# A two-block network on one core: opening from free memory, gate products with the input moving, gate rows through DRAM, alternating banks

## The chip, the cores and the metric

The kernel is one program on one core of a Trainium2 chip. The metric is the time of the whole launch in microseconds (us), the median of several runs. Engines are named as in the profile: PE (TensorE matmul), DVE (VectorE), ACT (ScalarE), POOL (GpSimd), SP (SyncE, which here issues most of the loads). A row of the profile that begins with `ACTq` or `SPq` is a transfer that this engine issues.

## The reference

One sequence of S=512 tokens with D=1024 features goes through two blocks of two layers each, all in float32. Heads, softmaxes and recurrences are left out here; what matters is where linears, modulations and gates stand.

```
cs = silu(c)
ada = cs @ w_ada[i] + b_ada[i]                # 6 vectors of 1024 per layer
sh1, sc1, g1, sh2, sc2, g2 = split(ada, 6)
u = x * (1 + sc1) + sh1
proj = u @ m_w_in                             # q, k (2048), v, o (1024 each), 8 gate columns
y = mlstm(conv and silu of qk, v, o, gates) @ m_w_out
x = layer_norm(alpha * x + (1 + g1) * y)
u = x * (1 + sc2) + sh2
y = (gelu(g) * a) @ f_w_down                  # a, g = conv(u @ f_w_up), 2 * 2816 columns
x = layer_norm(alpha * x + (1 + g2) * y)
# then a second layer like it, with differential attention in place of the mLSTM cell
# second block: its own c_2, mod_w, mod_b; x = x + (1 + gt) * y with rms_norm ahead of each half
#   layer 0: RWKV7 time mix (r, k, v from three mixes of the same input), then a squared-relu MLP
#   layer 1: shared k, v and 16 gate columns, forgetting attention, then a squared-relu MLP
```

## The kernel before

Each engine has a program of its own, written out in order by hand; the only thing that moves work between them is semaphores (`wait_ge`). The stages follow each other as m (mLSTM), f0 (its feed-forward net), d (differential attention), f1, r (RWKV7), g0 (MLP), x (forgetting attention), g1 (MLP).

**Linears.** Weights come as tiles of 1 MB through three slots (`ring`), issued by SP, which waits for `used` of the tile three before. Each tile is split in two parts, `w_high` by ACT (`act_split`) and `w_low` by DVE (`dve_split`), two tiles ahead (`AHEAD = 2`). A product is three matmuls of 128x512 (high by high, high by low, low by high). A *turn* is two tiles of one linear: 96 such matmuls into banks 0 to 3 of PSUM. In a linear of kind "f" (`pe_linear_f`) the weight is the stationary side and the four sums of a turn come out one after another; in one of kind "t" (`pe_linear_t`) all four come out in the last piece. `act_evict`, `dve_beside`, `dve_residual` and `act_residual` are what ACT and DVE do in a turn; in all of them the split of the last piece stands behind the turn's evictions or residual.

**Modulation blocks.** `c @ w_ada` is 52 blocks of 1024x512 ("ada"), 2 MB each through two buffers (`ada_ring`). DVE multiplies and adds the eight row groups into `ada_acc` and adds the bias row, on one partition; PE then sums over partitions with four products of one column (`pe_ada`), and ACT copies four columns into `mod` (`act_ada`). Most blocks stand beside a turn. The first four stand ahead of everything in `ada_first`; the "1 +" of a scale is added by DVE in `dve_modulate`.

**Turned inputs.** `pe_turn` transposes the input into banks 4 to 7, ACT scales and shifts it into `stage`, and ACT and DVE write `u_high` and `u_low`.

**Gate products.** The 8 gate columns of m and the 16 of x are made by `pe_gates` between the turned input and the first linear: the input is the stationary side and 8 or 16 columns move, and the sums are transposed afterwards.

**Gate rows.** The residual needs `1 + g` as a row on all partitions. `pe_gate_rows` makes it with eight products of a broadcast column by the identity in front of each of the eight inputs that follow (m out, f0, d out, f1, r out, g0, x out, g1), and `dve_gate_rows` copies it with 1 added.

**Joins.** Between the stages, `join` makes every engine wait until all others have come to it.

Of the kernel before, what the change touches and what calls it, by code (L numbers as in the profile page):

```python
# [9 lines left out]
F32 = mybir.dt.float32  # L10
F32R = mybir.dt.float32r
# [3 lines left out]
P = 128  # L15
# [26 lines left out]
def shape_constants():  # L42
# [40 lines left out]
    ("c", 8), ("c_2", 8), ("m_conv_b", 16), ("m_norm_g", 8), ("d_norm_g", 8), ("norm_mix_g_2", 16),  # L83
    ("norm_mlp_g_2", 16), ("kv_norm_g_2", 8), ("f_conv_b", 88), ("m_conv_w", 64), ("rw_mu_2", 48),
    ("f_conv_w", 264),
]

# [34 lines left out]
class Queue:  # L122
# [60 lines left out]
    def dma_start(self, out, in_):  # L183
        return self.e.dma_start(out, in_) if self.live else QUIET
# [18 lines left out]
class Linear:  # L203


    def __init__(self, name, kind, w, turns, at, kts=KT, r0=0, ada=None):
# [5 lines left out]
        self.first = None  # L212
# [12 lines left out]
class Net:  # L225
    def __init__(self, nc, ctx, args, out, scratch):
        self.nc, self.a, self.out, self.scratch = nc, args, out, scratch
# [4 lines left out]
        self.ada_row_in = Signal(nc, "ada_row_in")  # L232
# [9 lines left out]
        self.signals = [self.T, self.V, self.A, self.G, *self.weights_in, *self.ada_in, self.ada_row_in,  # L242
                        self.params_in, self.core_in, self.x_in, self.stage_in, self.wkv_par_in,
# [5 lines left out]
    def layout(self):  # L249
# [19 lines left out]
        self.arow = take("ada_bias_row", [1, 512])  # L269
# [7 lines left out]
        self.rows = take("param_rows", [P, 5, P])  # L277
        ar.top = base
        self.stage = take("stage", [P, 2, S])
        self.u = [take(f"u_{x}", [P, KT, S], F32R) for x in ("high", "low")]  # L280
        lin = ar.top

# [5 lines left out]
        self.m_gw = self.gate_tiles("m", 8)  # L288
# [72 lines left out]
        self.x_gw = self.gate_tiles("x", 16)  # L361
# [12 lines left out]
    def gate_tiles(self, s, n):  # L374
        take = self.ar.take
        return [take(f"{s}_gw_raw", [P, KT, n]), take(f"{s}_gw_nat", [P, TT, n]),
                take(f"{s}_gw_high", [P, KT, n], F32R), take(f"{s}_gw_low", [P, KT, n], F32R)]
# [6 lines left out]
    def linears(self):  # L384
        a = self.a
        ada = {"a0": (a["w_ada"][0], a["b_ada"][0], 0, self.cs[:, 0:8]),
               "a1": (a["w_ada"][1], a["b_ada"][1], 48, self.cs[:, 0:8]),
               "m0": (a["mod_w_2"][0], a["mod_b_2"][0], 96, self.cs[:, 8:16]),
               "m1": (a["mod_w_2"][1], a["mod_b_2"][1], 144, self.cs[:, 8:16]),
               "kv": (a["kv_mod_w_2"], a["kv_mod_b_2"], 192, self.cs[:, 8:16])}  # L390
        self.ada_blocks = []

        def blocks(which, b0, n):
            w, b, col, cs = ada[which]
            first = len(self.ada_blocks)
            self.ada_blocks += [(w[:, (b0 + i) * 512:(b0 + i + 1) * 512], b[(b0 + i) * 512:(b0 + i + 1) * 512],
                                 col + 4 * (b0 + i), cs) for i in range(n)]
            return list(range(first, first + n))
# [37 lines left out]
        at = 0  # L436
        for x in lin:
            x.first = at
            at += x.turns * len(x.pieces)
        self.lin = {x.name: x for x in lin}  # L440
        self.weights = [tile for x in lin for tile in x.tiles()]
        self.break_at = self.lin["r_out"].first

# [32 lines left out]
    def sync_program(self, sp):  # L476
        a = self.a
        sp.dma_start(self.ident_t[:], a["core_constants"]).then_inc(*self.core_in.landed("core"))
        at = 0
        for name, n in COLUMN_PARAMS:  # L480
            src = self.row(name).rearrange("(r f) -> r f", f=P)
            done = 0
            while done < n:
                t, r = divmod(at, P)
                m = min(n - done, P - r)
                sp.dma_start(self.rows[r:r + m, t, :], src[done:done + m, :]).then_inc(*self.params_in.landed("rows"
                             if at + m == self.ncols else at))
                done += m
                at += m
        for b in self.ada_first:  # L490
            self.sp_ada(sp, b)
# [23 lines left out]

    def sp_linear(self, sp, name):
        L = self.lin[name]
        tiles = list(L.tiles())
# [2186 lines left out]
```

## Time and profile before

| | |
|---|---|
| median of 3 runs | 3668.22 us (3659.37 to 3672.21) |
| the profiled execution, own time | 3660.21 us |
| its span in the trace | 3658.9 us |
| PE busy | 3179.2 us, 87% of the span |
| DVE busy | 2089.3 us, 57% |
| ACT busy | 1121.9 us, 31% |
| mean granted clock of PE | 0.918 |
| bytes moved | 341.35 MB, mean 93 GB/s |

The span is from the first instruction to the last. The granted clock is a share of full speed: 1.00 is 2.4 GHz and 0.50 is 1.2 GHz. What is not PE's busy time, some 480 us, is idle time of PE between instructions.

### The profile page before, as it was taken

What the parts mean: (1) busy time and instruction counts of PE and PEld (TensorE: products, weight loads), DVE (VectorE), ACT (ScalarE), POOL (GpSimd) and SP (SyncE); (2) the same over time, 40 slices, a digit from 0 to 9 for tenths busy, and PEclk for the clock granted to TensorE, in tenths of its full rate; (3) what the DMA queues carried; (4) which work ended last, traced back from release to release, by engine and by line L of the source; (5) the groups of instructions that cost most, each with busy time, mean ns of one, the idle gap of its engine ahead of it and who ended that gap; (6) DMA issues with size and microseconds to landing.
All of it is one profiled execution on the core that took longest, in us unless ns stands there. A gap on an engine that the chain in (4) does not pass through costs nothing.

```text
span 3658.9 us, 46712 instructions
## 1 busy us (share of the span) xinstructions
PE 3179.2 (87%) x19829; PEld 2572.1 (70%) x19829; DVE 2089.3 (57%) x3089; ACT 1121.9 (31%) x1823; POOL 175.4 (5%) x137
## 2 busy tenths in 40 slices
PE   3989799996978799994978777689998998979998
PEld 3776688875845588872757677468887876768886
DVE  4655787776546686866346767345353153545353
ACT  1233242222234232322323434132123143433121
POOL 0000100001000100001003322000000001100000
PEclk8899899998979899997988998789999898989999
DMA  5552344643510354541210000113232121012332
GB/s 179 138 138 92 114 158 146 207 140 132 186 38 12 104 184 161 184 156 30 81 54 12 8 11 8 45 46 93 92 104 82 58 82 45 1 47 81 104 93 86
DMA packets 226684, 341.35 MB, mean 93 GB/s; under 512 B 11128, under 2 KB 113200, under 8 KB 226476
## 3 DMA queue, kind: packets, MB, share of 16 engines
q1 hardware_dynamic: 217484, 326.79, 27.7%
q10 hardware_dynamic: 8992, 11.58, 1.0%
q8 instruction: 156, 2.56, 0.3%
q14 instruction: 52, 0.43, 0.0%
HBM read 336.22 MB, written 2.12 MB: 92 GB/s over the span
## 4 chain that ended last, share of the span: by engine, by line
PE 70%; DVE 19%; ACT 6%; DMA 3%; issue 2%; SPq 0%; POOL 0%; ACTq 0%; DVEq 0%; POOLq 0%
PE bank L139 68%; DVE w_tiles L148 4%; DVE ada_acc L160 3%; PE bank L142 2%; DVE w_low L148 2%; DVE x_natural L148 1%; ACT w_high L145 1%; DVE m_acc L160 1%; ACT stage L145 1%; ACT small L145 1%; DMA weight_ring<-in_m_w_in 1%; DVE stage L148 1%; DVE u_low L148 1%; DVE w_g L148 1%; DVE f_g L160 0%
## 5 line engine op out<-in xcount | busy, mean ns | idle before, releaser
L148 DVE TENSOR_TENSOR w_low<-weight_ring,w_high 128x2048 fp32r<-128x2048 f32 (+2 forms) x212 | 463.1, 2189 | 573.5 <-ACT w_high L145 573.5
L139 PE MATMUL bank<-u_high,w_high 128*128 128x512 f32 x1472 | 580.1, 394 | 7.4 <-DVE w_low L148 7.1
L139 PE MATMUL bank<-u_low,w_high 128*128 128x512 f32 x1472 | 575.7, 391 | 0.0
L139 PE MATMUL bank<-u_high,w_low 128*128 128x512 f32 x1472 | 575.4, 391 | 0.0
L145 ACT ACTIVATE w_high<-weight_ring 128x2048 fp32r<-128x2048 f32 (+2 forms) x212 | 387.5, 1829 | 524.5 <-DMA weight_ring<-in_mlp_down 155.9
L139 PE MATMUL bank<-w_high,u_high 128*128 128x512 f32 x896 | 356.8, 398 | 23.6 <-ACT u_high L145 14.3
L139 PE MATMUL bank<-w_low,u_high 128*128 128x512 f32 x896 | 353.7, 395 | 0.0
L139 PE MATMUL bank<-w_high,u_low 128*128 128x512 f32 x896 | 353.3, 394 | 0.0
L139 PEld LDWEIGHTS bank<-u_high,w_high 128*128 128x128 f32 x1472 | 277.9, 189 | 67.2 <-DVE w_low L148 7.3
L139 PEld LDWEIGHTS bank<-u_high,w_low 128*128 128x128 f32 x1472 | 278.1, 189 | 59.2
L139 PEld LDWEIGHTS bank<-u_low,w_high 128*128 128x128 f32 x1472 | 278.3, 189 | 56.9
L160 DVE SCALAR_TENSOR_TENSOR ada_acc<-ada_ring,silu_c,ada_acc 128x512 f32<-128x512 f32 x364 | 273.7, 752 | 17.0 <-DMA ada_ring<-in_w_ada 0.9
L139 PEld LDWEIGHTS bank<-w_high,u_high 128*128 128x128 f32 x896 | 171.2, 191 | 65.3 <-DVE u_low L148 19.6
L139 PE MATMUL bank<-w_tiles 64*64 64x64 f32 (+1 forms) x4224 | 179.9, 243 | 36.4 <-ACT w_tiles L145 21.5
L139 PEld LDWEIGHTS bank<-w_tiles 64*64 64x64 f32 x4224 | 166.0, 152 | 51.0 <-ACT w_tiles L145 22.5
L139 PE MATMUL bank<-w_high,g_hidden_high 128*128 128x512 f32 x512 | 199.2, 389 | 0.0
L139 PE MATMUL bank<-w_low,g_hidden_high 128*128 128x512 f32 x512 | 199.2, 389 | 0.0
L139 PE MATMUL bank<-w_high,g_hidden_low 128*128 128x512 f32 x512 | 199.2, 389 | 0.0
L139 PEld LDWEIGHTS bank<-w_high,u_low 128*128 128x128 f32 x896 | 171.2, 191 | 36.6
L139 PEld LDWEIGHTS bank<-w_low,u_high 128*128 128x128 f32 x896 | 171.4, 191 | 34.7
L139 PE MATMUL bank<-w_high,f_hidden_high 128*128 128x512 f32 x352 | 139.0, 395 | 6.7 <-DVE w_low L148 4.1
L139 PE MATMUL bank<-w_high,f_hidden_low 128*128 128x512 f32 x352 | 137.2, 390 | 0.0
(370 smaller groups left out, 4671.6 us busy)
## 6 DMA issues: line engine op xcount, KB each, us to landing
ada_ring<-in_w_ada SPq DMA_DIRECT2D x48, 1024.0 KB, 7.9
ada_ring<-in_mod_w SPq DMA_DIRECT2D x48, 1024.0 KB, 7.5
weight_ring<-in_f_w_up SPq DMA_DIRECT2D x44, 1024.0 KB, 5.1
weight_ring<-in_mlp_up SPq DMA_DIRECT2D x32, 1024.0 KB, 5.5
weight_ring<-in_mlp_down SPq DMA_DIRECT2D x32, 1024.0 KB, 5.0
weight_ring<-in_f_w_down SPq DMA_DIRECT2D x24, 768.0 KB, 4.4
weight_ring<-in_m_w_in SPq DMA_DIRECT2D x16, 1024.0 KB, 9.6
weight_ring<-in_d_w_in SPq DMA_DIRECT2D x12, 1024.0 KB, 5.2
```

What stands on the lines that cost most here:

```text
L139: return self.e.matmul(out, l, r, start=start, stop=stop, skip_group_check=True)
L142: return self.e.transpose(out, in_, ident) if self.live else QUIET
L145: return self.e.activation(out, in_, f, **kw) if self.live else QUIET
L148: return self.e.tensor_tensor(out, a, b, op) if self.live else QUIET
L160: return self.e.scalar_tensor_tensor(out=out, in0=a, scalar=s, in1=b, op0=op0, op1=op1)
```

## The change

Six things are changed together.

1. *The opening.* The first four modulation blocks get 8 MB of memory of their own (`first_ada`), which later stages use again. SP loads blocks 0 and 2, then the small parameters, weight tile 0, blocks 1 and 3, weight tile 1. Blocks 0 and 1 are multiplied on PE (32 products of one column each), blocks 2 and 3 summed on DVE. The first half of the input is turned between them. Biases and layer-norm vectors join the parameters that come in by columns, and the "1 +" is put in them once.
2. *Biases.* A bias is added to four columns by DVE when it takes the sum from the bank (`dve_ada_take`), in place of the one-partition row operation, its load, and ACT's copy.
3. *Gate products.* The gate weights are the stationary side and the input moves (512 columns): 24 matmuls, put between the first and the second turn of m_v and x_k.
4. *Gate rows.* ACT stores the eight columns to DRAM (`act_gate_store`) and later loads them back on all partitions, 512 KB (`act_gate_load`). Nothing of them is left on PE or DVE; `dve_residual` waits for the load.
5. *Banks.* Turns take banks 0 to 3 and 4 to 7 by turns (`group`), and the turned input takes all eight.
6. *Orders.* The last split of a turn stands ahead of its residual or evictions; the silu of m_qk comes one bank later; in the feed-forward nets gelu and hidden parts come after both splits of a turn; the mix of the next input of the r linears is made while the linear before still runs.

```diff
+    def pe_first_block(self, pe, b):
+        pe.wait_ge(self.A, "silu")
+        if b == 1:
+            pe.wait_ge(self.V, "first", 0)
+        for j in range(4):
+            for k in range(KT):
+                pe.wait_ge(self.first_in[b][k // 4], "first")
+                m = pe.matmul(self.bank[6][:, 4 * b + j:4 * b + j + 1], self.first_w[:, b, k, j * P:(j + 1) * P], self.cs[:, k:k + 1],
+                              k == 0, k == KT - 1)
...
+    def dve_ada_take(self, v, b):
+        _, bias, at, _ = self.ada_blocks[b]
+        v.wait_ge(self.T, "ada", b)
+        v.tensor_tensor(self.mod[:, at:at + 4], self.bank[self.ada_bank.get(b, 7)][:, 0:4], bias, ALU.add).then_inc(
...
+    def act_gate_store(self, a, st):
+        col = GATES[st]
+        self.modulated(a, col, 8)
+        dst = self.gate_rows[list(GATES).index(st)].rearrange("(j p) -> p j", p=P)
+        a.dma_start(dst, self.mod[:, col:col + 8], True).then_inc(*self.gates_out.landed())
+
+    def act_gate_load(self, a, st, tile):
+        a.wait_ge(self.gates_out)
+        src = self.gate_rows[list(GATES).index(st)].partition_broadcast(P)
+        a.dma_start(tile, src).then_inc(*self.gates_in.landed(st))
...
+    def pe_gates(self, pe, s, bank, rows, tiles):
+        _, high, low = tiles
         pe.wait_ge(self.V, "gate parts", s)
...
+        for f in range(KT):
+            m = self.product(pe, self.bank[bank][0:rows, :], [y[:, f, :] for y in (high, low)], [x[:, f, :] for x in self.u],
+                             f == 0, f == KT - 1)
...
     def act_residual(self, a, name, squares=False):
         L = self.lin[name]
         for i in range(L.turns):
             self.act_ahead_all(a, name, i)
+            self.act_ahead(a, name, i, len(L.pieces) - 1)
             if squares:
...
+    def r_passed(self, q, before, f):
+        if before:
+            q.wait_ge(self.T, "used", self.lin[before].tile(1, f // 4))
```

How instructions move, at three places. First PE at the start of the program, up to the first product of m_qk (`first_ada` is the free memory, `first_acc` the sums of blocks 2 and 3, `x_natural` the input). Before, with the gate products' first rows:

```order
L142 MATMUL bank<-core_constants,param_rows 128x128 x4
L142 MATMUL bank<-core_constants,param_rows 128x40
L139 MATMUL bank<-ones,ada_acc 128x1 x16
L142 MATMUL bank<-core_constants,x_natural 128x128 x32
L139 MATMUL bank<-m_gw_high,u_high 128x8
```

Now:

```order
L144 MATMUL bank<-core_constants,param_rows 128x128
L141 MATMUL bank<-silu_c,first_ada 128x1 x32
L141 MATMUL bank<-ones,first_acc 128x1 x4
L144 MATMUL bank<-core_constants,x_natural 128x128 x16
L144 MATMUL bank<-core_constants,param_rows 128x128 x5
L144 MATMUL bank<-core_constants,param_rows 128x56
L141 MATMUL bank<-silu_c,first_ada 128x1 x32
L141 MATMUL bank<-ones,first_acc 128x1 x4
L144 MATMUL bank<-core_constants,x_natural 128x128 x16
L141 MATMUL bank<-u_high,w_high 128x512
```

The 64 products with `first_ada` are new on PE, the input is turned in two halves, and no gate product stands ahead of m_qk any more.

Second DVE in a turn of the feed-forward net f0 (`f_a` and `f_g` are the two convolved halves). Before:

```order
L148 TENSOR_TENSOR w_low<-weight_ring,w_high 128x2048
L160 SCALAR_TENSOR_TENSOR f_g<-bank,param_columns,f_g 128x511
L160 SCALAR_TENSOR_TENSOR f_g<-bank,param_columns,f_g 128x510
L148 TENSOR_TENSOR f_g<-f_g,f_a 128x512
L163 CAST f_hidden_high<-f_g 128x512
L148 TENSOR_TENSOR f_hidden_low<-f_g,f_hidden_high 128x512
L160 SCALAR_TENSOR_TENSOR f_g<-bank,param_columns,f_g 128x511
```

Now:

```order
L150 TENSOR_TENSOR w_low<-weight_ring,w_high 128x2048
L162 SCALAR_TENSOR_TENSOR f_g<-bank,param_columns,f_g 128x511
L162 SCALAR_TENSOR_TENSOR f_g<-bank,param_columns,f_g 128x510
L162 SCALAR_TENSOR_TENSOR f_g<-bank,param_columns,f_g 128x511
L162 SCALAR_TENSOR_TENSOR f_g<-bank,param_columns,f_g 128x510
L150 TENSOR_TENSOR w_low<-weight_ring,w_high 128x2048
L150 TENSOR_TENSOR f_g<-f_g,f_a 128x512
L165 CAST f_hidden_high<-f_g 128x512
L150 TENSOR_TENSOR f_hidden_low<-f_g,f_hidden_high 128x512
```

Both splits now stand ahead of the hidden parts, which used to stand between them.

Third PE between the turned input of x and the linear x_k. Before, the end of the 96 gate products:

```order
L139 MATMUL bank<-x_gw_high,u_high 128x16
L139 MATMUL bank<-x_gw_low,u_high 128x16
L139 MATMUL bank<-x_gw_high,u_low 128x16
L142 MATMUL bank<-core_constants,x_gw_nat 16x128 x4
L139 MATMUL bank<-w_high,u_high 128x512
```

Now, at the end of x_k's first turn:

```order
L141 MATMUL bank<-w_high,u_high 128x512
L141 MATMUL bank<-w_low,u_high 128x512
L141 MATMUL bank<-w_high,u_low 128x512
L141 MATMUL bank<-u_high,x_gw_high 16x512
L141 MATMUL bank<-u_low,x_gw_high 16x512
L141 MATMUL bank<-u_high,x_gw_low 16x512
```

x_k now starts right behind the turned input, and 24 gate products stand behind its first turn.

## Rows read from the trace of the kernel before

**Rows 1.** The page: busy time, share of the span and instructions of each engine

```profile
PE 3179.2 (87%) x19829; PEld 2572.1 (70%) x19829; DVE 2089.3 (57%) x3089; ACT 1121.9 (31%) x1823; POOL 175.4 (5%) x137
```

**Rows 2.** Who PE waited for, whole run: total us, times, longest

```profile
PE bank L139 <- DVE ada_acc L148: 55.7, 9, 11.2
PE bank L139 <- DVE x_natural L148: 33.4, 2, 19.0
PE bank L139 <- DVE w_low L148: 29.2, 10, 6.4
...
PE bank L142 <- ACT stage L145: 20.2, 12, 13.9
...
PE bank L139 <- ACT u_high L145: 14.3, 2, 7.1
```

**Rows 3.** Stretches: length, busy us (x) of PE PEld DVE ACT POOL, clock, DMA share, GB/s

```profile
0.00:99.00 99.00, 38.58 (x174) 35.59 (x174) 40.51 (x64) 14.47 (x21) 0.20 (x4) 0.79 0.54 165
5.00:10.00 5.00, 0.00 (x0) 0.00 (x0) 0.00 (x0) 0.00 (x0) 0.00 (x0) 1.00 1.01 351
99.00:315.00 216.00, 193.04 (x839) 159.48 (x838) 131.26 (x148) 68.43 (x79) 0.00 (x0) 0.93 0.57 156
463.00:845.00 382.00, 375.38 (x1702) 309.40 (x1701) 296.71 (x362) 116.17 (x125) 0.00 (x0) 1.00 0.49 168
2467.00:2815.00 348.00, 348.00 (x1538) 288.15 (x1537) 152.07 (x164) 85.28 (x83) 0.00 (x0) 1.00 0.30 94
```

**Rows 4.** PE in order of time, 0 to 104 us: start, duration, idle before and releaser

```profile
11.37 1.34 PE L142 MATMUL bank<-core_constants,param_rows 128*128 128x128 f32 x5 [11.37 <-DMA param_rows<-in_f_conv_w]
...
48.18 1.87 PE L139 MATMUL bank<-ones,ada_acc 128*128 128x1 f32 x8 [7.29 <-DVE ada_acc L148]
...
67.49 4.05 PE L142 MATMUL bank<-core_constants,x_natural 128*128 128x128 f32 x16 [13.94 <-ACT stage L145]
...
98.97 0.80 PE L139 MATMUL bank<-u_high,w_high 128*128 128x512 f32 x1
```

**Rows 5.** DMA issues: KB each, median us from issue to landing

```profile
weight_ring<-in_f_w_up SPq DMA_DIRECT2D x44, 1024.0 KB, 5.1
weight_ring<-in_m_w_in SPq DMA_DIRECT2D x16, 1024.0 KB, 9.6
```

**Rows 6.** DVE in m_qk's first turn, and beside the join behind m_o

```profile
100.20 5.55 DVE L160 SCALAR_TENSOR_TENSOR ada_acc<-ada_ring,silu_c,ada_acc 128x512 f32<-128x512 f32 x7
105.85 0.68 DVE L148 TENSOR_TENSOR ada_acc<-ada_acc,ada_bias_row 1x512 f32<-1x512 f32 x1
...
112.04 2.31 DVE L160 SCALAR_TENSOR_TENSOR m_acc<-bank,param_columns,m_acc 128x511 f32<-128x511 f32 x3 [3.09 <-ACT m_acc L145]
...
312.08 2.29 DVE L148 TENSOR_TENSOR w_low<-weight_ring,w_high 128x2048 fp32r<-128x2048 f32 x1 [9.02 <-ACT w_high L145]
```

**Rows 7.** Groups of instructions, whole run: busy us, mean ns, idle before

```profile
L139 PE MATMUL bank<-core_constants,modulation_columns 128*128 128x128 f32 x128 | 29.4, 422 | 68.0 <-DVE x_natural L148 33.4 <-DVE w_low L148 12.9 <-DVE d_o L148 7.5
L139 PE MATMUL bank<-x_gw_high,u_high 128*128 128x16 f32 x32 | 11.6, 362 | 5.4 <-DVE x_gw_low L148 5.4
```

**Rows 8.** PE in order of time, around the starts of g0 and x_k

```profile
2453.39 3.45 PE L139 MATMUL bank<-core_constants,modulation_columns 128*128 128x128 f32 x16 [6.44 <-DVE w_low L148]
2460.70 6.57 PE L142 MATMUL bank<-core_constants,g_xn 128*128 128x128 f32 x32 [3.86 <-ACT g_xn L145]
...
2826.92 6.09 PE L142 MATMUL bank<-core_constants,x_q 128*128 128x128 f32 x32 [11.44 <-ACT x_q L145]
2838.36 0.38 PE L139 MATMUL bank<-x_gw_high,u_high 128*128 128x16 f32 x1 [5.35 <-DVE x_gw_low L148]
...
2860.65 0.80 PE L139 MATMUL bank<-w_high,u_high 128*128 128x512 f32 x1 [0.77 <-DVE x_f L163]
```

**Rows 9.** ACT and DVE at the end of m_out (DVE's residual began at 427.44)

```profile
427.89 1.92 ACT L145 ACTIVATE w_high<-weight_ring 128x2048 fp32r<-128x2048 f32 x1 [9.64 <-DMA weight_ring<-in_f_w_up]
...
436.26 2.27 DVE L148 TENSOR_TENSOR w_low<-weight_ring,w_high 128x2048 fp32r<-128x2048 f32 x1
```

More of the change, by code:

```diff
@@ L435, in linears @@
         lin += mlp(1)
-        at = 0
+        at = turn = 0
+        self.ada_bank = {}
         for x in lin:
-            x.first = at
+            x.first, x.turn0 = at, turn
             at += x.turns * len(x.pieces)
+            turn += x.turns
+            for i, b in enumerate(x.ada or ()):
+                self.ada_bank[b] = 7 - x.group(i)
         self.lin = {x.name: x for x in lin}
@@ L442, in linears @@
         self.break_at = self.lin["r_out"].first
+        after = {"m u": "m_qk", "m o u": "m_out", "f0": "f0_up0", "d u": "d_qk", "d o u": "d_out", "f1": "f1_up0",
+                 "r o u": "r_out", "g0": "g0_up0", "x kv": "x_k", "x q": "x_q", "x o u": "x_out", "g1": "g1_up0"}
+        self.turn_group = {st: self.lin[name].group(0) for st, name in after.items()}
     def row(self, name):
@@ L833, in dve_gates, with dve_gate_parts @@
-    def dve_gates(self, v, s, n, outs, rows, tiles):
-        raw, nat, high, low = tiles
+        if bank in self.free:
+            pe.wait_ge(*self.free[bank])
+        for f in range(KT):
+            m = self.product(pe, self.bank[bank][0:rows, :], [y[:, f, :] for y in (high, low)], [x[:, f, :] for x in self.u],
+                             f == 0, f == KT - 1)
+        m.then_inc(*self.T.up("gate sums", s))
+        self.free[bank] = (self.V, "gates out", s)
+    def dve_gate_parts(self, v, s, parts, tiles):
+        raw, high, low = tiles
+        if len(parts) > 1:
+            v.memset(high[:].bitcast(F32), 0.0).then_inc(*self.V.up())
+            v.memset(low[:].bitcast(F32), 0.0).then_inc(*self.V.up())
@@ L835, in dve_gates @@
         v.wait_ge(self.stage_in, "gate w", s)
-        v.tensor_copy(high[:], raw[:]).then_inc(*self.V.up())
         v.wait_ge(self.V)
-        v.tensor_tensor(low[:], raw[:], high[:].bitcast(F32), ALU.subtract).then_inc(*self.V.up("gate parts", s))
-        for t in range(TT):
-            v.wait_ge(self.T, "gate sums", s, t)
-            v.tensor_copy(nat[:, t, :], self.bank[4 + t][:, 0:n]).then_inc(*self.V.up("gate nat", s, t))
-        for j, (out, c0) in enumerate(outs):
-            v.wait_ge(self.T, "gates turned", s, j)
-            v.tensor_copy(out, self.bank[j][0:rows, :]).then_inc(*self.V.up("gates out", s, j))
+        for c0, n, at in parts:
+            v.tensor_copy(high[:, :, at:at + n], raw[:, :, c0:c0 + n]).then_inc(*self.V.up())
@@ new lines, in dve_gate_parts, with dve_gates_out @@
+        v.wait_ge(self.V)
+        for c0, n, at in parts:
+            v.tensor_tensor(low[:, :, at:at + n], raw[:, :, c0:c0 + n], high[:, :, at:at + n].bitcast(F32), ALU.subtract).then_inc(
+                *self.V.up())
+        self.V.mark("gate parts", s)
+    def dve_gates_out(self, v, s, bank, outs):
+        v.wait_ge(self.T, "gate sums", s)
+        for out, at, n in outs:
+            v.tensor_copy(out, self.bank[bank][at:at + n, :]).then_inc(*self.V.up())
+        self.V.mark("gates out", s)
@@ new lines, in dve_first_sums @@
+    def dve_first_sums(self, v, b):
+        acc = self.first_acc[:, b - 2, :]
+        v.wait_ge(self.A, "silu")
+        for k in range(KT):
+            src, col = self.first_w[:, b, k, :], self.cs[:, k:k + 1]
+            v.wait_ge(self.first_in[b][k // 4], "first")
+            if k == 0:
+                v.tensor_scalar(acc, src, col, None, ALU.mult).then_inc(*self.V.up())
+            else:
+                v.wait_ge(self.V)
+                v.scalar_tensor_tensor(acc, src, col, acc, ALU.mult, ALU.add).then_inc(*self.V.up())
+        self.V.mark("first summed", b)
```

571 lines of the change are left out of this document (312 added, 259 removed).

## The prediction

> **What bounds the kernel now.** I read the page first: PE is busy 87% of the span [rows 1], so PE's order sets the time, and what can be won is its idle time of some 480 us, its slow stretches and work that can leave it. Then who PE waited for [rows 2]: DVE almost everywhere (ada_acc 55.7 us, x_natural 33.4, w_low 29.2), with ACT's stage 20.2 and u_high 14.3. Then the stretches [rows 3]. In the MLP g0 PE is busy 348.00 of 348.00 us and in f0 375.38 of 382.00, at clock 1.00: nothing is to be had there. The opening is the opposite, 38.58 of 99.00 us. From m_qk to the end of m_o it is 193.04 of 216.00 at clock 0.93. So I cost the change from stage to stage and make the sum against the profiled execution's own time, 3660.2 us; the median of the runs shown is 8.0 us above it.
>
> **The opening, -43.** Now DVE sums four blocks one after another until 50 us, PE waits 13.94 us for the first turned input because both splits stand ahead of it, and 96 thin gate products follow; m_qk starts at 98.97 [rows 4]. After, PE's own chain is: parameters 11 (the wait now is 11.37), block 0 with 32 products that run as 64 passes (8 instructions for 4 products in 1.87 us, 0.234 each) 15, the summed block 1, taking it 2, half the input 4, the other parameters 1.5, block 1 15, then 1, 2 and 4 again: 56.5 us [rows 4]. The loads need 6.3 MB at 351 GB/s [rows 3], 18 us, then 9.6 for a tile of m_w_in [rows 5], then 4.2 MB, 12 us: 39.6 us, and some 9 behind it for sum, take and half a turn. So 56 is PE's, if its thin products run at 1.2 GHz as they do now. Bounds: at 2.4 GHz both blocks take half, and the loads' 48 decides; with parameters and blocks landing 7 us later, 63.
>
> **m_qk to the cell, -24.** This is 215.5 us now (98.97 to 314.4, where DVE's last split ends) for 8 turns [rows 3, 6]. g0 ran 1538 matmuls in 348.00 us, 0.226 each, so a turn of 96 with its ada product is 22.7 [rows 3]; 8 of them are 181.6, 24 gate products 5.5, a cold start 2: 189. The waits inside come from DVE: ada 5.55 + 0.5, a bias row 0.68, 12 convolution steps of 0.77, two splits of 2.29, and waits like 3.09 for ACT's answer [rows 6]: 20.9 busy plus some 6 of waiting is over 22.7. Without the bias row, and with ACT's silu a bank later, it is 20.2 and few waits. But the gate chain of m now stands right ahead of m_o on DVE, and each turn loads two slow tiles and a 2 MB block: 2 x 8 + 6 = 22 us at the measured speeds, just as long as PE's turn. I take 2 us for these, 191. Bounds: 188.5, and 200 if every turn waits for its loads.
>
> **Gate rows, -29.** 128 products, 16 a place at 8 places, 29.4 us busy and 3.45 in such a place [rows 7]. Each stands behind a join, where nothing covers it. At r out and the two MLP starts DVE's copies stand in the chain as well: g0's turned input starts 7.31 us after its gate rows, 4.1 of it theirs [rows 8]. So 5 x 3.4 + 3 x 4.1 = 29. What takes their place on ACT is 8 stores and 8 loads of 512 KB; a load is issued at the join, and the first sums of the linear come more than half a turn, 11 us, behind its start, so I cost them at nothing. If that cover were gone, a load of 512 KB plus its way is about half a tile's 5.1 us [rows 5].
>
> The rule that speaks against it: the Trainium skill (DMA: Bandwidth & Descriptors, Specifications) says that a transfer of less than 512 B makes the DMA engine read, change and write back, and the stores here are 1024 pieces of 4 B each. No row of before shows such a store. By the rows the sum has nothing for it; by the rule it would be the rival on stores below, 3564.
>
> **Gate products, -24 more.** Only those of x; m's are in the opening. From the end of x's turned input (2833.0) to x_k it is 27.6 us: 5.35 waiting for the gate weights' split, then 22.3 for 96 products, transposes and a copy [rows 7, 8]. After: 24 x 0.226 = 5.4 behind the first turn, and x_k's first 5 us, now at 1.2 GHz, come 2 cheaper. -24; bound -19, if the clock is still low where x_k starts.
>
> **Last splits ahead, joins, -8.** PE waited 29.2 us for w_low in 10 places, 6.44 in each of r out and x out [rows 2, 8]. At d_v and x_gate the split of an already landed tile leaves the join: 1.9 of ACT and 2.3 of DVE less, -4 each (m_o's is counted). In linears with a residual DVE meets the split first and the residual later: in m_out the tile landed at 427.87, ACT's part takes 1.92, DVE's 2.27, so the residual starts at 432.1 and not 427.44, and its 8.9 us end at 441, against 438.5 for the split now [rows 9]: +2.4. The same in d_out +2.8; in the other five it is a gain of about 1 each. Together zero.
>
> **r linears, -8.** PE waits 14.3 us in two places for u_high [rows 2], because mixing starts when the linear has ended. After, it stands behind the last split, whose tile lands some 9 us into the last half of 11; the first mixes are then just late: about 3 us of each 7.1 stay. Bounds -4 and -14.
>
> **The rest, -8.** Turned x q: up to 6 us of waits for stage with all eight banks [rows 2], I take -3 (bound 0). Small waits in f0 and f1, which total 6.6 in f0 [rows 3]: -5. 52 bias rows are hidden elsewhere: DVE has 297 of 382 us busy in f0. Nothing is late for them.
>
> Sum: -43 -24 -29 -24 -8 +0 -8 -8 = -144: 3660 - 144 = 3516 for a profiled execution, and 8 more for a median: 3524.
>
> **The rivals.**
> - *The loads or the thin products hold the first stages (0.15).* The opening ends at 63 and m's turns take 24 us each because m_w_in's tiles take 9.6 us [rows 5]. +7 +9, with r linears and x q at their bounds +7: about 3547. For it: DMA at 0.57 share in a stretch where PE waits. Against: 156 GB/s is far from 351.
> - *DVE's new order stalls PE (0.08).* With the residual behind a split that waits for its tile, and hidden parts late, turns of f0, f1 and the outs wait 1 us in 40 places: 3565.
> - *More is won (0.12).* PE's opening at 2.4 GHz (-8), DMA never late (-2), r linears whole (-6), x q (-3): 3505 and less.
> - *The other side: slower (0.03).* The 22 up turns of the feed-forward nets pass the point where DVE fits: a split that comes after PE wants it stretches the turn. To eat 144 us each must stretch by 6.5 us. In f0 DVE is idle for 85 us of 382 [rows 3], 5.0 in each of 17 turns, so its waits for gelu would have to grow by 11.5 us in a turn; 2 ACT answers of 3.09 [rows 6] are far from that.
> - *The gate stores cost (0.05).* By a mechanism here: 1024 pieces each hold the 16 DMA engines while weights are due. m_qk's first DVE wait or a late tile would show it: 8 stores x up to 5 us, a tile's time [rows 5], on the path, is 40: 3564. Were the rule of the Trainium skill quoted above to decide, it would be this case.
> - *It wins nothing (0.02)*: everything removed would have to be given back, 3655 to 3668. Gate rows and gate products stand on PE behind waits, so they can't have been hidden.
>
> The rest, 0.55, is the forecast, with its own range 3508 to 3540. The range for 8 in 10 goes from 3495 (the opening at its bound and more won) to 3568 (DVE's order, the stores). Under 0.3% (11 us) a measurement here can't tell from no change: faster 0.95, same 0.02, slower 0.03.
>
> **What would show it.** m_qk's first product at 48 to 63 us, with 32 products of block 0 beginning near 11 and taking 15; the cell's start 188 to 200 us behind; no row with modulation_columns on PE; x_k starting within 1 us of the turned input; PE's waits for u_high in r under 8 us in all; g0's turned input 3 us behind its join. Wrong it would be if DMA showed a share near 1 for long in the opening, if gates_in were what ends a wait of DVE's residual, or if f0's stretch from the first to the last product grew from 382 us.

## The result and the profile after

The changed kernel takes 3574.05 us (median of 4 runs, 3568.2 to 3576.78), the kernel before 3666.2 us (4 runs, 3659.37 to 3672.21): a ratio of 0.9747, 95% interval 0.9725 to 0.9769. That is faster by 92 us, where 144 were forecast, and the time lies 6 us above the range. The profiled execution took 3573.32 us with a span of 3572.0, which is 86.9 below the span before.

The page of the changed kernel, busy time by engine, to be read beside [rows 1]:

```profile
PE 3154.2 (88%) x19659; PEld 2546.2 (71%) x19659; DVE 2037.4 (57%) x3045; ACT 1111.3 (31%) x1771; POOL 175.4 (5%) x137
```

Who PE waited for, whole run, beside [rows 2]:

```profile
PE bank L144 <- DVE x_natural L150: 62.0, 3, 25.2
PE bank L144 <- ACT r_r L147: 32.3, 1, 32.3
PE bank L141 <- DMA w_wa<-in_rw_a: 25.1, 1, 25.1
...
PE bank L141 <- DVE ada_acc L162: 23.0, 7, 13.7
...
PE bank L141 <- DVE modulation_columns L150: 16.4, 7, 4.7
...
PE bank L141 <- DVE u_low L150: 10.7, 15, 3.1
...
PE bank L141 <- DVE w_low L150: 4.4, 1, 4.4
```

w_low fell from 29.2 to 4.4 us, ada_acc from 55.7 to 23.0, and u_high in the r linears is gone. Three names are new or have grown: a DMA that brings `w_wa` (25.1, it was 7.8 before), `modulation_columns`, which is DVE's new instruction that takes a modulation sum from its bank, and `u_low` (10.7, it was 3.8).

Stretches of the changed kernel, beside [rows 3]: the opening, from there to the cell, f0, g0.

```profile
0.00:56.10 56.10, 39.79 (x182) 38.84 (x183) 20.94 (x36) 9.73 (x13) 0.20 (x4) 0.82 0.96 288
56.10:244.40 188.30, 187.53 (x859) 154.01 (x857) 133.33 (x160) 70.49 (x76) 0.00 (x0) 1.00 0.66 175
380.50:776.20 395.70, 385.00 (x1736) 317.76 (x1736) 291.02 (x366) 118.81 (x118) 0.00 (x0) 0.98 0.48 166
2397.00:2751.70 354.70, 354.45 (x1568) 293.54 (x1568) 155.25 (x166) 89.99 (x84) 0.00 (x0) 0.99 0.29 92
```

From m_qk to the cell PE is now busy 187.53 of 188.30 us at clock 1.00. f0 is the other kind: 10.7 us of PE idle in its 395.7.

PE in order of time in the opening, beside [rows 4]:

```profile
7.38 0.45 PE L144 MATMUL bank<-core_constants,param_rows 128*128 128x128 f32 x1 [7.38 <-DMA param_rows<-in_m_conv_b]
8.55 1.87 PE L141 MATMUL bank<-silu_c,first_ada 128*128 128x1 f32 x8 [0.72 <-ACT silu_c L147]
13.10 12.11 PE L141 MATMUL bank<-silu_c,first_ada 128*128 128x1 f32 x56 [2.69 <-DMA first_ada<-in_w_ada]
25.85 1.87 PE L141 MATMUL bank<-ones,first_acc 128*128 128x1 f32 x8 [0.65 <-DVE first_acc L162]
27.58 3.65 PE L144 MATMUL bank<-core_constants,x_natural 128*128 128x128 f32 x16
31.03 1.47 PE L144 MATMUL bank<-core_constants,param_rows 128*128 128x128 f32 x6
36.69 1.83 PE L141 MATMUL bank<-silu_c,first_ada 128*128 128x1 f32 x8 [4.19 <-DMA first_ada<-in_w_ada]
39.21 12.11 PE L141 MATMUL bank<-silu_c,first_ada 128*128 128x1 f32 x56 [0.69 <-DMA first_ada<-in_w_ada]
...
56.14 0.48 PE L141 MATMUL bank<-u_high,w_high 128*128 128x512 f32 x1
...
78.00 0.95 PE L141 MATMUL bank<-ones,ada_acc 128*128 128x1 f32 x8
```

The granted clock can't be read from its column at the start. It says 1.00 until 32 us and 0.50 from 36 to 56 us, but 56 instructions with `first_ada` take 12.11 us in both places, and eight with `first_acc` 1.87 and 1.84 us where the eight like them at 78.00, at clock 1.00, take 0.95. By these durations PE's thin products ran at 1.2 GHz in the whole opening, and its mean of 0.82 above is too high.

The table sets the whole change out by stages. Each stage runs from the start of the first PE instruction of its name to that of the next, read from the time-ordered rows of the two first traces; the forecast column is the prediction's own terms put in their stages (they sum to -144).

| stage | before | after | change | forecast |
|---|---|---|---|---|
| start to m_qk | 98.97 | 56.14 | -42.8 | -43 |
| m_qk to cell | 215.50 | 188.31 | -27.2 | -24 |
| cell to m_out's turned input | 69.51 | 63.47 | -6.0 | -3.4 |
| m_out, to f0's turned input | 73.11 | 72.60 | -0.5 | -1.0 |
| f0 | 413.47 | 420.85 | **+7.4** | -3.4 |
| d u to d heads | 165.80 | 162.96 | -2.8 | -4 |
| d heads | 149.62 | 145.90 | -3.7 | -3.4 |
| d_out | 79.51 | 80.20 | +0.7 | -0.6 |
| f1 | 421.66 | 433.94 | **+12.3** | -3.4 |
| r u to r_r | 48.73 | 49.18 | +0.5 | 0 |
| r_r to wkv | 161.02 | 167.34 | **+6.3** | -8 |
| wkv to r_out's turned input | 501.08 | 494.62 | -6.5 | -4.1 |
| r_out | 62.72 | 61.48 | -1.2 | -5.1 |
| g0 | 366.22 | 365.24 | -1.0 | -1 |
| x's turned input to x heads | 230.85 | 200.88 | -30.0 | -31 |
| x heads | 168.55 | 180.27 | **+11.7** | -3.4 |
| x_out | 64.17 | 60.23 | -3.9 | -5.1 |
| g1 and end | 368.40 | 368.40 | 0.0 | 0 |

The large terms came as forecast. Two rows can't be read to the microsecond, because they differ between executions of one kernel: the d heads (149.62 and 156.20 us in two traces of the kernel before) and wkv (494.6, 492.0 and 497.8 in three of the changed one). Four stages, in bold, moved the wrong way, and miss the forecast by 10.8, 15.7, 14.3 and 15.1 us: 56 of the 57 us that are lacking.

PE at the starts of g0 and x_k, beside [rows 8]:

```profile
2396.99 1.30 PE L144 MATMUL bank<-core_constants,g_xn 128*128 128x128 f32 x5 [9.19 <-ACT g_xn L147]
...
2762.23 5.65 PE L144 MATMUL bank<-core_constants,x_q 128*128 128x128 f32 x32 [10.54 <-ACT x_q L147]
2767.64 0.49 PE L141 MATMUL bank<-w_high,u_high 128*128 128x512 f32 x1
```

x_k starts 0.2 us before the modelled end of the turned input, and no gate row stands ahead of g0's input.

**Where f0 and f1 lose.** PE's two rows in f1's last down linear, and DVE's at the same place:

```profile
1529.38 0.50 PE L141 MATMUL bank<-w_high,f_hidden_high 128*128 128x512 f32 x1 [2.73 <-DVE modulation_columns L150]
1564.18 0.50 PE L141 MATMUL bank<-w_high,f_hidden_high 128*128 128x512 f32 x1 [4.71 <-DVE modulation_columns L150]
```

```profile
1553.32 1.75 DVE L150 TENSOR_TENSOR w_low<-weight_ring,w_high 128x1536 fp32r<-128x1536 f32 x1
1555.17 0.69 DVE L150 TENSOR_TENSOR stage<-bank,f_gate_rows 128x512 f32<-128x512 f32 x1
...
1563.98 0.14 DVE L150 TENSOR_TENSOR modulation_columns<-bank,param_columns 128x4 f32<-128x4 f32 x1
```

The modulation sum of a turn is written into the last bank of the other group (`ada_bank` is 7 minus the group), and that is the fourth bank of the next turn. PE needs it after three quarters of the next turn's first piece, which in the second down linear (10 row groups) is 4.4 us. DVE frees it with an instruction of 0.14 us that stands behind a whole residual of 8.9 us. Of that lateness the split ahead of the residual is 1.75 us.

**Where the start of wkv loses.** ACT's and SP's transfers there (start, time from the first to the last issue):

```profile
1814.05 2.39 ACTq L186 DMA_DIRECT2D gate_rows<-modulation_columns  x2
1816.53 0.54 ACTq L186 DMA_DIRECT2D w_const<-in_wkv_constants  x1
```

```profile
1816.94 0.43 SPq L186 DMA_DIRECT2D w_par<-in_rw_rk  x1
1817.42 8.38 SPq L186 DMA_DIRECT2D w_wa<-in_rw_w  x2
1825.84 1.51 SPq L186 DMA_DIRECT2D w_wa<-in_rw_a  x2
```

```profile
1820.00:1825.00 5.00, 0.00 (x0) 0.00 (x0) 0.00 (x0) 0.00 (x0) 0.00 (x0) 0.50 0.07 2
1825.00:1830.00 5.00, 0.00 (x0) 0.00 (x0) 0.00 (x0) 0.00 (x0) 0.00 (x0) 0.50 0.93 23
```

SP needs 8.38 us for two issues. The last two numbers of a stretch are the busy share of the DMA engines and GB/s: for five microseconds they are 0.07 and 2, then 0.93 and 23. ACT's two stores of 4 KB stand ahead of them, on another queue.

### The profile page after: what moved, and what is told of

Read it like the earlier page. It is cut to its first block, busy times and chain, and to the rows that moved or that the text cites. A ratio compares the mean times of both kernels' runs of the same rounds, so it can differ in the third digit from the quotient of the medians.

```text
span 3572.0 us, 46213 instructions
## 1 busy us (share of the span) xinstructions
PE 3154.2 (88%) x19659; PEld 2546.2 (71%) x19659; DVE 2037.4 (57%) x3045; ACT 1111.3 (31%) x1771; POOL 175.4 (5%) x137
## 4 chain that ended last, share of the span: by engine, by line
PE 73%; DVE 15%; DMA 4%; ACT 4%; issue 1%; SPq 1%; POOL 0%; ACTq 0%; DVEq 0%; POOLq 0%
PE bank L141 71%; DVE w_tiles L150 4%; PE bank L144 3%; DVE w_low L150 2%; DVE x_natural L150 2%; DVE ada_acc L162 1%; ACT w_high L147 1%; SPq L186 1%; DVE stage L150 1%; DMA weight_ring<-in_f_w_down 1%; ACT small L147 1%; ACT stage L147 1%; DMA weight_ring<-in_d_w_in 0%; DVE u_low L150 0%; DVE w_g L150 0%
## 5 line engine op out<-in xcount | busy, mean ns | idle before, releaser
L141 PE MATMUL bank<-w_high,u_high 128*128 128x512 f32 x896 | 353.7, 395 | 14.3 <-DVE u_low L150 9.7
L162 DVE SCALAR_TENSOR_TENSOR ada_acc<-ada_ring,silu_c,ada_acc 128x512 f32<-128x512 f32 x336 | 252.6, 752 | 15.2
L141 PEld LDWEIGHTS bank<-w_tiles 64*64 64x64 f32 x4224 | 163.0, 150 | 50.9 <-ACT w_tiles L147 22.4
L141 PE MATMUL bank<-w_high,f_hidden_high 128*128 128x512 f32 x352 | 142.7, 405 | 16.4 <-DVE modulation_columns L150 16.4
L141 PE MATMUL bank<-w_low,f_hidden_high 128*128 128x512 f32 x352 | 140.4, 399 | 0.0
```

The costliest lines, as they stand in the source:

```text
L141: return self.e.matmul(out, l, r, start=start, stop=stop, skip_group_check=True)
L162: return self.e.scalar_tensor_tensor(out=out, in0=a, scalar=s, in1=b, op0=op0, op1=op1)
```

## The experiments

All ratios are against the kernel before, run beside it on the same chip. Of each kernel's executions one was traced, and stage times are from that one.

### The stores of g0 and g1 behind the wkv stage

```diff
-        for gate in ("g0", "g1"):
-            self.act_gate_store(a, gate)
         self.join(a, self.A, "r wkv start")
...
         self.act_gate_load(a, "r", self.r_gb[:])
+        for gate in ("g0", "g1"):
+            self.act_gate_store(a, gate)
```

> The changed kernel with the two gate stores of g0 and g1 moved from the start of the wkv stage to behind it. Theory A (a store of 1024 pieces of 4 bytes holds the DMA queues for about 9 us, and the small loads of the wkv stage that are issued behind it come late): PE's wait for w_wa at the start of wkv falls from 25.1 us to about 8, and the time by 17 us, to about 3557. Theory B (the small loads are late for another reason, such as the earlier end of the linears before them): that wait stays near 25 and the time near 3574.

3553.29 us, ratio 0.9678 (0.9642 to 0.9714). The way from r_r to wkv is 148.06 us and not 167.34. SP's two issues and PE's wait with late stores:

```profile
1818.35 1.00 SPq L186 DMA_DIRECT2D w_wa<-in_rw_w  x2
```

```profile
PE bank L141 <- DMA w_wa<-in_rw_a: 7.3, 1, 7.3
```

Theory A holds: 19.3 us are the stores'. The traced execution took 3534.96 us, the other three 3549.24 to 3560.08; the section on the x heads comes back to this.

### Stores of 32 bytes

```diff
-        dst = self.gate_rows[list(GATES).index(st)].rearrange("(j p) -> p j", p=P)
+        dst = self.gate_rows[list(GATES).index(st)].rearrange("(p j) -> p j", p=P)
...
+                g3 = gates.rearrange("q (p j) -> q j p", j=8)[:, 4 * i:4 * i + 4, :]
```

> The changed kernel with each gate stored as 128 pieces of 32 bytes (the 8 columns of a partition together) in place of 1024 pieces of 4 bytes; the row is loaded in that order, and the residual reads it with a stride of 8 elements. Same bytes, an eighth of the pieces. Theory A (the number of pieces holds the queues): a store lands in about 2 to 3 us and not 9 to 14, the wait for w_wa falls to about 9 us, the wait of 4.8 us at the end of f1's first down turn vanishes, and the time falls by 18 to 22 us, to about 3554. Theory B (the wait is for a store to DRAM as such, not for its pieces): stores still take 9 us or more and the time stays within 4 of 3574. A side that may cost: the strided read makes the residual's product slower than 0.69 us.

3567.16 us, ratio 0.9727 (0.9702 to 0.9753). The stores' rows of the changed kernel and of this one, with the median us to landing:

```profile
gate_rows<-modulation_columns ACTq DMA_DIRECT2D x8, 4.0 KB, 11.8
```

```profile
gate_rows<-modulation_columns ACTq DMA_DIRECT2D x8, 4.0 KB, 3.5
```

The same 4 KB land in 3.5 us as 128 pieces and in 11.8 as 1024, and the way from r_r to wkv is 149.63 us. So it is the pieces, not the store to DRAM as such; whether it is their number or their size is not told apart, since both changed by a factor of 8. The wait of 4.79 us for ada_acc at the end of f1's first down turn, some 30 us behind a store, is gone as well. The Trainium skill (DMA: Bandwidth & Descriptors, Specifications) says that below 512 B the engine reads, changes and writes back. No run here shows that mechanism; the trace agrees that pieces of 4 B are slow, and shows that being below 512 B is not all of it, since 32 B are too. The total gained only 7 us, because the side that may cost did cost:

```profile
L150 DVE TENSOR_TENSOR stage<-bank,f_gate_rows 128x512 f32<-128x512 f32 x32 | 35.5, 1108 | 3.3
```

A product that reads its second operand with a stride of 8 elements takes 1.11 us and not 0.69. Each turn with a residual ends later on DVE, and the wait for modulation_columns grows from 16.4 to 22.4 us.

### The take of the modulation sum first

```diff
             self.dve_ahead(v, name, i, len(L.pieces) - 1)
+            if L.ada and i < L.turns - 1:
+                self.dve_ada_take(v, L.ada[i])
             for t in range(TT):
...
-            if L.ada:
+            if L.ada and i == L.turns - 1:
                 self.dve_ada_take(v, L.ada[i])
```

In the up linears of the feed-forward nets the take moves likewise ahead of the hidden parts.

> The changed kernel with the modulation sum taken from its bank ahead of the residual (all turns but a linear's last) and ahead of the hidden parts. Theory A (the wait of 16.4 us in 7 places is the next turn's fourth bank, which still holds the modulation sum because DVE takes it last): the four longest of these waits, 4.3, 2.7, 4.7 and 2.7 us, vanish, and the time falls by 14 to 15 us, to about 3560. Theory B (DVE is late there because the split stands ahead of the residual, and the wait only moves to the residual or the split): PE waits as long for DVE under another name, and the time falls by less than 4.

3550.44 us, ratio 0.9682 (0.9652 to 0.9712). f0 takes 409.43 us and f1 420.05, so 11.4 and 13.9 less. All that is left under that name is

```profile
PE bank L144 <- DVE modulation_columns L150: 0.3, 1, 0.3
```

Theory A holds and was sized too low: 25.3 us in the two stages, where the waits for modulation_columns were 16.4. Of the other 9, 2.5 are the wait for ada_acc at f1's first down turn, which falls from 4.79 to 2.27 us. Part of the rest is PE's clock behind a stall: in the changed kernel it is 0.60 from 1564 to 1568 us, right behind the wait of 4.71. With the takes mended f0 is 4.0 and f1 1.6 us shorter than in the kernel before, where 3.4 each were forecast.

### The last split behind the residual

```diff
-            self.dve_ahead(v, name, i, len(L.pieces) - 1)
             for t in range(TT):
...
+            self.dve_ahead(v, name, i, len(L.pieces) - 1)
             if L.ada:
                 self.dve_ada_take(v, L.ada[i])
```

> The changed kernel with the last split of a turn behind the residual again, on ACT and DVE, in the linears with a residual (one of the order changes undone). Theory A (bank and take): the residual starts some 1.8 us sooner and the take 0 to 1 us sooner, so the waits for modulation_columns stay above 12 us; the tails of m_out and d_out are 2 to 3 us shorter each, those of the other five 1 us longer: within 4 us of 3574. Theory B (split ahead of the residual is what costs): the waits of 16.4 us fall below 5 us, to about 3562.

3558.95 us, ratio 0.9714 (0.968 to 0.9748). The waits for modulation_columns stay at 16.3 us, f0 at 420.47, f1 at 435.43: theory B falls. m_out and d_out are 3.1 and 3.0 us shorter, as their tails were costed. The traced execution is 16.1 us below the changed kernel's, and the x heads alone are 16.6 below (163.71 us, see below). That the median, 15 us lower, is theirs too is likely and not shown.

### One group of banks

```diff
-        return 4 * ((self.turn0 + i) % 2)
+        return 0
...
-        return (self.turn_group[st] + f) % 8
+        return f if st == "m u" else 4 + f % 4
```

> The changed kernel with the alternating banks undone: sums always in banks 0 to 3, modulation sums in bank 7, turned inputs in banks 4 to 7. Theory A (the 16.4 us of waits for modulation_columns exist only because a modulation sum shares a bank with the next turn): they are 0, but PE then waits for DVE's residual at the start of each turn, since the residual now begins at the turn's end; f0 and f1 stay within 8 us of 421 and 434. Theory B (alternation is what hides evictions everywhere, and worth more than it costs): the time rises by more than 20 us, to 3595 or more, most in m_qk and the turns with residuals.

3588.87 us, ratio 0.9764 (0.9729 to 0.98), in runs from 3566 to 3599. The waits for modulation_columns are gone but for 0.3 us, and PE waits for DVE's residual instead:

```profile
PE bank L141 <- DVE stage L150: 11.4, 12, 1.9
```

f0 and f1 take 420.47 and 431.36 us, so theory A holds for them; the median is 14.8 us above the changed kernel's, less than theory B's 20. Elsewhere alternation is worth 4.8 us from r_r to wkv and 3.6 in r_out, and nothing from m_qk to the cell (188.90). The other 12 and 7 us, in wkv and the d heads, are stages that vary with the clock from one execution to another.

### Three fixes together

Late stores, takes first, and DVE's last split behind the residual in the last turns of m_out and d_out alone (ACT's stays ahead).

> The changed kernel with the late stores of g0 and g1, the early takes, and the last split of m_out and d_out behind the residual as before. Theory A (the three are independent losses on PE's path): by stages, the way from r_r to wkv is 148 us, f0 409 and f1 420, m_out and d_out 3 us shorter each; together 19 + 25 + 6 = 50 below the changed kernel, near 3524, or 3510 to 3540 with the granted clock of the x heads. Theory B (they overlap, since a stage that ends earlier only waits longer for the same loads): less than 35 in sum.

3524.61 us (3520.11 to 3527.84), ratio 0.9609 (0.9593 to 0.9624). By stages r_r to wkv, f0 and f1 take 148.28, 414.17 and 418.07 us; m_out and d_out are 1.1 and 2.5 us shorter. That is 45 us by stages and 49.4 by medians, nearer to theory A's 50 than to theory B's 35: the losses overlap little. In f0 only 6.7 of the 11.4 us came. That 3524, the prediction's number for the change, is reached with three orders mended is a coincidence, since it was added up without them and the x heads still take 180.32 us.

### The gate products of x in front

```diff
-        self.pe_linear_t(pe, "x_k", self.u, self.A, u="x kv",
-                         between=lambda: self.pe_gates(pe, "x", self.lin["x_k"].group(1) + 2, 16, self.x_gw))
+        pe.wait_ge(self.V, "u", "x kv", KT - 1)
+        self.pe_gates(pe, "x", self.lin["x_k"].group(1) + 2, 16, self.x_gw)
+        self.pe_linear_t(pe, "x_k", self.u, self.A)
```

DVE copies the sums there too, ahead of x_k's turns.

> The changed kernel with the 24 gate products of x ahead of x_k, where the 96 stood before, and their copy taken there. Theory A (the 22 us saved at x come from the shape, 24 matmuls of 512 columns for 96 of 16, and not from the place): the way from x's turned input to the x heads is 2 to 4 us longer than the 201 of the changed kernel, by the wait for the gate weights' split. Theory B (the place counts as much): it is 8 us longer or more.

3573.6 us, ratio 0.9736 (0.9709 to 0.9763). The way from x's turned input to the x heads is 208.0 us: 22.8 below the kernel before, 7.1 above the changed one, between the two theories and nearer to B. Of the 7.1, PE's wait for the split of the gate weights is 5.97:

```profile
2768.58 0.58 PE L141 MATMUL bank<-u_high,x_gw_high 128*16 128x512 f32 x1 [5.97 <-DVE x_gw_low L150]
```

The 22.8 us are not all the shape's: 5.0 of them lie behind x_v, in the turned input x q and the join behind x_gate. From x's turned input to that of x q the kernel before takes 123.4 us, this one 105.6 and the changed one 98.2. So the shape brings some 18 us and the place 7. The traced execution took 3557.97 us, with 163.70 in the x heads, the other three 3569.8 to 3578.56.

### The x heads

The x heads are the same instructions in all kernels here. Stretches that cover them from the first score, in the kernel before, the changed kernel and the one with late stores:

```profile
3058.70:3216.50 157.80, 152.18 (x861) 112.54 (x859) 81.38 (x229) 65.67 (x201) 16.28 (x14) 0.94 0.00 1
```

```profile
2964.00:3137.10 173.10, 167.54 (x861) 124.37 (x860) 81.37 (x229) 65.89 (x201) 16.30 (x14) 0.85 0.00 1
```

```profile
2942.80:3099.40 156.60, 150.90 (x858) 111.45 (x856) 81.42 (x230) 65.66 (x201) 16.29 (x14) 0.95 0.00 1
```

DVE and ACT are busy for the same time; PE's clock is 0.94, 0.85 and 0.95. What differs is how long the clock is low at the stage's start (at 3057.77, 2963.11 and 2941.86 us). In the same order:

```profile
3053.90:3077.50 23.60, 16.77 (x52) 11.76 (x53) 10.52 (x18) 5.51 (x15) 5.88 (x5) 0.50 0.00 0
```

```profile
2960.90:3015.30 54.40, 49.23 (x159) 36.17 (x160) 19.17 (x44) 13.46 (x40) 6.83 (x6) 0.50 0.05 18
```

```profile
2943.00:2959.80 16.80, 13.92 (x40) 9.28 (x41) 6.90 (x13) 5.25 (x14) 2.37 (x2) 0.50 0.00 1
```

Behind each of these stretches the clock is 1.00 almost to the stage's end. It is low for 54 us where it fell 2 us ahead of the stage's start, in PE's wait, and for 17 where it fell 1 us behind it. The first experiment puts products of constants in PE's two waits at the stage's start:

```diff
+        for _ in range(5):
+            pe.matmul(self.bank[0][:], self.ident, self.ident_t[:], True, True)
         self.pe_x_turned(pe, 0)
+        for _ in range(3):
+            pe.matmul(self.bank[0][:], self.ident, self.ident_t[:], True, True)
```

> The same kernel with 8 products of the constants (128x512, float32, no result used) in the two waits of PE at the start of the x heads, five in the first and three in the second. Theory A (the x heads take 164 or 180 us by how long the clock stays at 1.2 GHz behind these idle stretches): with PE busy through them the stage takes 164 us or less each time, and the median is 8 or more us below the kernel without them. Theory B (the clock's time at 1.2 GHz there has nothing to do with the two waits): the median is the same or up to 3 us above it.

3516.12 us (3504.88 to 3521.53), ratio 0.9582 (0.956 to 0.9605), 8.5 below the kernel without them. The stage takes 157.28 us, less than in any other kernel, at clock 1.00 (the medians differ by less than the stage's 23 us; in the two traces the d heads and wkv, which lie ahead of the added products, took 7.7 and 12.0 us longer):

```profile
2935.20:3086.00 150.80, 147.50 (x868) 108.77 (x866) 81.43 (x230) 65.52 (x201) 16.29 (x14) 1.00 0.00 1
```

Then the two kernels once more, as they are:

> The changed kernel as it is, once more. Theory A (the x heads' time hangs on how long the clock happens to stay low in an execution): this execution or the next shows 164 us and not 180 for the stage, with no instruction changed, while the stages r_r to wkv and f1 repeat within 2 us (167 and 434). Theory B (it belongs to the changed kernel): 180 both times.

> The changed kernel as it is, a third execution with a trace, for the same question: 164 or 180 us for the x heads (theory A: either, by chance; theory B: 180).

> The kernel before, as it is, a second execution with a trace. If the x heads' 168.6 us of the first trace belong to that kernel, this one shows 167 to 170 again, and the 12 us that the changed kernel loses there (180.3 in three executions) come from the change; if it shows 180 or 164, the stage varies by itself and the 12 us are chance. The d heads (149.6) and the wkv stage with the gate (501.1) are read for the same question.

The changed kernel took 3569.08 and 3576.65 us, with 180.35 us for the x heads both times; the kernel before 3668.18, with 168.60. So the sign that theory A of the first two asked for did not come: three traces of the changed kernel and two of the kernel before repeat the stage to 0.1 us. That does not exclude chance. The late stores' traced execution took 3534.96 us with 163.72 in this stage and its other three 3549 to 3560, and `long_wait_late` below, the same kernel but for one split, took 3553.24 with 179.94. The kernel with gates in front spreads the same way. Whether one kernel can show both sizes is open. The last pair gives the changed kernel its longer wait back:

```diff
+            if name != "x_gate":
+                self.act_ahead(a, name, i, len(L.pieces) - 1)
...
+            if name == "x_gate":
+                self.act_ahead(a, name, i, len(L.pieces) - 1)
```

> The changed kernel with ACT's last split of x_gate behind its evictions again (for this linear alone), so that PE's wait at the start of the x heads is 8.4 us as before, and not 4.3. Theory A (the 168.6 us of the kernel before against 180.3 and 163.7 come from how long PE was idle ahead of the stage): the x heads take 168 to 169 us. Theory B (it is where the stage lies in the execution, or something behind the wait): 180 or 164.

> The same with the late stores of g0 and g1, which moves the stage by 20 us. Theory A: 168 to 169 us again. Theory B: another of the three sizes.

One execution each, 3574.15 and 3553.24 us. PE's wait ahead of the stage is 8.45 us in both, as in the kernel before (8.44), and the x heads take 179.94 and 179.94. Theory A fell: the length of that wait alone does not pick the size.

### More products of constants in PE's waits

Five and 13 of them around the wait for d_bias, 15 in the wait for r's gate weights, besides the 8 of the x heads.

> The kernel with three fixes and the 8 products at the start of the x heads, and more such products of constants (results unused) in three other long waits of PE: 5 and 13 around the wait for d_bias, 15 in the wait for r_g2b behind the wkv stage. Theory A (stretches with thin or waiting PE stay at 1.2 GHz because PE was idle before them): the 32 products of r's gate, 1.0 us each now, take 0.5 us each, 16 us less; the d heads take about 143 us and not 147 to 155; the median falls from 3516 to about 3498. Theory B (they stay slow for another reason): r's gate keeps its 32 us and the time stays within 3 us of 3516.

3492.59 us (3483.67 to 3501.13), ratio 0.952 (0.9496 to 0.9545): 177 us below the kernel before, run beside it, and 81 below the changed one's median. r's gate in the changed kernel and here (each added product counts as two instructions):

```profile
2302.55 2.05 PE L141 MATMUL bank<-r_g2a,r_sg 128*128 128x512 f32 x2 [16.39 <-DMA r_g2b<-in_rw_g]
2304.52 2.07 PE L141 MATMUL bank<-r_g2b,r_sg 32*128 32x512 f32 x2
```

```profile
2235.46 14.71 PE L141 MATMUL bank<-core_constants 128*128 128x512 f32 x30 [9.27 <-DVE r_r L150]
2250.01 1.02 PE L141 MATMUL bank<-r_g2a,r_sg 128*128 128x512 f32 x2
2250.97 1.12 PE L141 MATMUL bank<-r_g2b,r_sg 32*128 32x512 f32 x2
```

A pair that took 2.05 us at a granted clock of 0.50 takes 1.02 to 1.12 at 1.00. From r's gate to r_out's turned input it is 17.7 us and not 33.0. The d heads take 137.47 us, where they took 145.9 to 156.2 in all other traces. Theory A holds.

## Why the prediction was right and where it failed

- **The opening, -43.** The mechanism is right: PE's chain sets it, 64 passes a block at 0.22 to 0.23 us, at 1.2 GHz by their durations. That it fits to 0.2 us is luck, because two errors cancel: parameters came at 7.4 us and not 11, and PE waited 2.69 and 4.19 us for blocks where the sum had no wait. One of the prediction's signs of being wrong did show: the DMA share is 0.96 for the whole opening, so the loads are nearly as tight as PE's chain.
- **m_qk to the cell, -24.** Right, 3 us low: the 2 us held back for the gate chain and slow tiles were not needed.
- **Gate rows, -29.** It is right about their place: from r's gate to r_out's turned input, where they stood, it is 7.1 us less (4.1 was forecast), and g0's turned input starts 4.6 us sooner behind the linear. In the d heads, wkv and x heads the clock's changes are larger than the term, so the whole -29 can't be read off. r_out gained 1.2 of 5.1. Ahead of it the gate rows had been the cover of the two splits behind the join: now DVE's 4.5 us of w_low stand between the turned input's first part and its low halves, and PE waits 1.98 us for u_low. This is read from the trace and was not tried.
- **Gate products, -24.** Right: 25.2 us from x's turned input to that of x q, some 18 by the shape and 7 by the place.
- **Last splits, 0; joins, -8.** The tails of m_out and d_out cost what was worked out (3.1 and 3.0 in the run that undoes them, for 2.4 and 2.8). The gain of about 1 us in each of the other five is 3.0 in all in that run. The joins brought 2.8 and 4.1.
- **x q, -3.** It brought some 0.7 us: the waits for stage of 1.41 and 2.26 are gone, but the next wait for w_low grew from 1.77 to 4.44.
- **r linears, -8.** Hidden in the table by the stores: with these late, the stage went from 161.02 to 148.06, -13.0, near the bound of -14. Of the two waits of 7.1 us for u_high one of 2.08 is left, now for u_low, and some of under 1. The mixes were less late than "about 3 us of each 7.1 stay".
- **What failed first: "so I cost them at nothing".** Said of the eight gate stores. Only the load's cover was weighed, not what queues behind the store on ACT and SP. At wkv nothing covers them: 19.3 us. The right mechanism stood among the rivals with 0.05, and the rule of the Trainium skill named there spoke for it. Its price was 8 x 5; it is 19 in one place, perhaps up to 4.8 in f1, and little in the others.
- **What failed second: "-5" for small waits in f0 and f1.** The sum spoke of DVE's busy time and named no bank, and the sign it gave for this showed: f0 from the first to the last product grew by some 9 us. Where the change moves an instruction, what it frees counts: the take of 0.14 us holds a bank that PE wants 4.4 us into the next turn. It cost 25.3 us. The rival on DVE's order (0.08) had put its stalls at the split, which one run excludes.
- **What failed third: nothing was said of the clock of stages that the change does not touch.** The x heads have -3.4 in the sum, for the gate rows, and took 11.7 us more. That it is the clock is shown (same instructions, same DVE and ACT time, low for 54 us and not 24 at the stage's start, and gone with PE kept busy). Why 168.6 became 180.3 stays open: the wait's length alone is excluded by two runs, and with the stage unchanged three variants gave 163.7 and the others 180.

## What to carry to other kernels

Before a small helper transfer is costed at nothing, count its pieces and list what is issued behind it on every queue: 1024 pieces of 4 bytes took 11.8 us, 128 of 32 bytes 3.5 (medians). When banks alternate, write down for each bank who frees it last and when it is wanted next; an instruction of 0.14 us at the end of a list cost more than all the splits that had been reordered. And where PE waits ahead of a long stage of thin products, a few products without a use in that wait can be worth more than the wait itself: 23 us by the traces for waits of 4.3 and 3.0 us ahead of the x heads.

## What the hardware showed that was not expected

- The clock behind an idle stretch: 32 instructions of r's gate ran at a granted clock of 0.50 for all of their 32 us, one behind the other, behind a wait of 16.4 us (16.7 in the kernel before, with the same result), and at 1.00 when the wait was filled. The x heads took 157 us filled and 164, 169 or 180 otherwise. The Trainium skill (TensorE: Matmul & The Clock Gate, Part 1) says that the slow start of one kernel differs between runs. It speaks of a kernel's start; of stages behind a wait, the d heads agree (149.6 and 156.2 us in one kernel), and the x heads did not differ in three traces of the changed kernel.
- A float32 product of DVE with one operand at a stride of 8 elements took 1.11 us for 0.69.
- Transfers issued by SP were held up behind ACT's stores on another queue: two issues in 8.38 us, for 1.00 with the stores moved away.
